# Blocks of 64 rows, high and low parts in one stationary operand, for an expert's rows beyond 128

## What is computed

```
eid = gid[:, None] * MOE_EXPERTS_PER_GROUP + top_i       # T x 2 experts
...
slot_tok = jnp.full((n_slots,), T, dtype=jnp.int32).at[dest].set(stok)
slot_w = jnp.zeros((n_slots,), jnp.float32).at[dest].set(sw)
...
def expert_block(args):
    toks, e = args
    xb = x_pad[toks]
    h = jax.nn.silu(xb @ w_eg[e]) * (xb @ w_eu[e])
    return h @ w_ed[e]
...
y = jnp.zeros((T + 1, D_MODEL), jnp.float32).at[slot_tok].add(out.astype(jnp.float32) * slot_w[:, None])
```

## Time and profile before

| what | value |
|---|---|
| median of 3 executions | 2094.23 us (2093.68 to 2094.96) |
| the profiled execution, its own time | 2093.3 us |
| its span in the profile | 2091.6 us |
| TensorE busy | 1989.5 us, 95% of the span |
| VectorE, ScalarE, GpSimd busy | 49%, 37%, 19% |
| mean granted TensorE clock | 0.983 of full |
| router's last part and experts | from 1618 us to the end |

### The profile page before, as it was taken

How to read it: one execution, slowest core, us unless ns; L and a number is a source line. 1 busy time by engine, 2 the same in 40 slices (tenths; PEclk the granted TensorE clock), 3 DMA queues, 4 the chain that set the end, 5 groups by cost and what they waited for, 6 DMA issues and landing times. The chain is left out here.

```text
span 2091.6 us, 33016 instructions
## 1 busy us (share of the span) xinstructions
PE 1989.5 (95%) x12316; PEld 1764.4 (84%) x12317; DVE 1014.6 (49%) x1166; ACT 776.2 (37%) x1109; POOL 398.2 (19%) x509
## 2 busy tenths in 40 slices
PE   7999999999999999898998999999999899999995
PEld 5788999999888888788997899888788788877884
DVE  4215255543656556465113431435534645784676
ACT  4322122222344344433002222423311456774684
POOL 2000100000444444350110000000000212232224
PEclk9999999999999999899999999999999999999998
DMA  6122233232334343496538021444316486998887
GB/s 197 61 89 68 70 90 94 81 91 82 105 118 125 107 131 103 144 318 236 178 124 278 21 71 30 151 162 162 113 71 224 136 272 194 361 381 270 296 289 278
DMA packets 247474, 333.01 MB, mean 159 GB/s; under 512 B 16269, under 2 KB 163629, under 8 KB 247329
## 3 DMA queue, kind: packets, MB, share of 16 engines
q1 hardware_dynamic: 211268, 276.25, 39.3%
q0 software_dynamic: 7344, 25.38, 4.7%
q10 hardware_dynamic: 28768, 30.02, 4.1%
HBM read 255.30 MB, written 77.61 MB: 159 GB/s over the span
## 5 line engine op out<-in xcount | busy, mean ns | idle before, releaser
L3877 ACT ACTIVATE e_w_high<-big 128x2048 fp32r<-128x2048 f32 x94 | 175.9, 1909 | 36.4 <-PEq L3012 18.0
L274 PE MATMUL psum<-hT_high,t_w_high 128*128 128x352 f32 x576 | 186.9, 324 | 0.3 <-DVE t_w_low L1017 0.3
L276 PE MATMUL psum<-hT_high,t_w_low 128*128 128x352 f32 x576 | 185.6, 322 | 0.0
L275 PE MATMUL psum<-hT_low,t_w_high 128*128 128x352 f32 x576 | 185.6, 322 | 0.0
L4004 DVE TENSOR_TENSOR e_w_low<-big,e_w_high 128x2048 fp32r<-128x2048 f32 x64 | 144.0, 2288 | 37.9 <-ACT e_w_high L3877 37.8
L3781 PE MATMUL psum<-e_w_high,e_xT_high 128*128 128x512 f32 x368 | 146.0, 397 | 8.3 <-issue 5.1
L3782 PE MATMUL psum<-e_w_low,e_xT_high 128*128 128x512 f32 x368 | 144.1, 392 | 0.0
L3783 PE MATMUL psum<-e_w_high,e_xT_low 128*128 128x512 f32 x368 | 144.1, 392 | 0.0
L274 PE MATMUL psum<-hT_high,s_w_high 128*128 128x352 f32 x384 | 131.3, 342 | 0.0
L275 PE MATMUL psum<-hT_low,s_w_high 128*128 128x352 f32 x384 | 124.2, 323 | 0.0
L276 PE MATMUL psum<-hT_high,s_w_low 128*128 128x352 f32 x384 | 124.1, 323 | 0.0
(11 more groups left out here) (570 smaller groups left out, 4885.2 us busy)
## 6 DMA issues: line engine op xcount, KB each, us to landing
big<-in_w_expert_gate SPq DMA_DIRECT2D x32, 1024.0 KB, 8.1
big<-in_w_expert_up SPq DMA_DIRECT2D x32, 1024.0 KB, 11.4
big<-in_w_expert_down SPq DMA_DIRECT2D x32, 1024.0 KB, 13.8
t_w<-in_w_in SPq DMA_DIRECT2D x24, 512.0 KB, 4.8
m_gates<-gate_scr SPq DMA_DIRECT2D x22, 528.0 KB, 5.7
x_scr<-t_conv_out ACTq DMA_DIRECT2D x20, 512.0 KB, 4.3
gate_scr<-s_gate_tanh ACTq DMA_DIRECT2D x16, 528.0 KB, 3.3
scan_w<-in_w_gate SPq DMA_DIRECT2D x16, 512.0 KB, 4.2
```

The lines of the kernel that those rows point to most:

```text
L274: nc.tensor.matmul(out, ah, w_h, start=start, stop=False)
L275: nc.tensor.matmul(out, ah, w_l, start=False, stop=False)
L276: return nc.tensor.matmul(out, al, w_h, start=False, stop=stop)
L3877: return nc.scalar.activation(dst, src, ACT.Copy)
```

## The change

Beyond its first 128 slots, an expert's slots now go in blocks of 64, which run ahead of the expert's full block. In such a block the 64 tokens sit in the even lanes. High and low parts of the turned rows lie in one tile `xhl` (128 x 8 x 2 x 128), and reading it with a step of 2 gives 128 stationary columns: 64 high, 64 low. So gate and up take 2 matmuls per contraction tile (with the high and with the low weights) in place of 3; PSUM then holds the high part's product in partitions 0 to 63 and the low part's in 64 to 127, and VectorE adds the two halves. The down product is unchanged. Experts 0 and 15 keep `hidden` for all of their blocks. The tables grow from 34 to 48 columns, since more blocks are possible. VectorE's `h_low` waits for the down parts in place of TensorE's `down`.

```diff
-NBLK = (2 * T + P - 1) // P + NE
+XR = 64
+NTHR = (T - P + XR - 1) // XR
+NBLK = NE + (2 * (T - P) + 2 * (XR - 1)) // XR + 1
...
-            ch.done(ts(nbk[:], nbk[:], 1.0, None, ALU.max))
-            ch.done(tt(low[:], low[:], mid(nbk[:], NE), ALU.mult))
+            nc.vector.tensor_copy(m.more[:], nbk[:])
+            ch.done(nc.vector.scalar_tensor_tensor(low[:], mid(nbk[:], NE), 1.0, low[:], ALU.add, ALU.mult))
...
+            ts(m.behind[:], base[:], -1.0, 0.0, ALU.add, ALU.max)
...
-        xh = g.sb("e_xT_high", [P, DK, P], F32R, ctx=ctx)
-        xl = g.sb("e_xT_low", [P, DK, P], F32R, ctx=ctx)
+        xhl = g.sb("e_xT", [P, DK, 2, P], F32R, ctx=ctx)
+        xh, xl = xhl[:, :, 0, :], xhl[:, :, 1, :]
...
-            with eng.Fori(0, NE - 1) as e:
-                expert(e, False)
+            expert(0, False, False)
+            with eng.Fori(1, NE - 1) as e:
+                expert(e, True, False)
             at_last()
-            expert(NE - 1, True)
+            expert(NE - 1, False, True)
...
+            def hidden_split(e, b):
+                pe.wait_ge(s_xl, b + 1)
+                pe.wait_ge(s_sg, b)
+                for bank, p, done in ((GA, 0, s_g), (UP, 2, s_u)):
...
+                        parts = xhl[:, k].rearrange("p a t -> p (a t)")[:, 0:2 * P:2]
+                        nc.tensor.matmul(ps[:, bank, :], parts, wh[:, p + half, at:at + BANK], start=(k == 0), stop=False)
+                        mm = nc.tensor.matmul(ps[:, bank, :], parts, wl[:, p + half, at:at + BANK], start=False,
+                                              stop=(k == DK - 1))
+                    mm.then_inc(done, 1)
+                turn(b + 1)
...
-            with pe.Fori(0, NE - 2) as e:
-
-                b = within(start(pe, e) + more(pe, e))
-                hidden(e + 1, b + 1)
-                down(e, b)
+            with pe.Fori(1, NE - 1) as e:
+
+                behind = pe.value_load(m.behind[0:1, bass.ds(e, 1)], min_val=0, max_val=NBLK)
+                n = more(pe, e)
+                with pe.If(n > 0):
+                    with pe.Fori(0, n) as i:
+                        b = within(behind + i)
+                        hidden_split(e, b + 1)
+                        down(b)
+                        turn_h(b + 1)
+                b = within(behind + n)
+                hidden(e, b + 1)
+                down(b)
                 turn_h(b + 1)
-                others(e + 1, b + 1, lambda b: down(e + 1, b))
...
+            def silu_split(b):
+                act.wait_ge(s_gs, b + 1)
+                nc.scalar.activation(sg[0:XR], sg[0:XR], ACT.Silu).then_inc(s_sg, 1)
...
             def gated(b):
+                for s in (s_gl, s_gs, s_ul, s_us):
+                    dve.sem_inc(s, 1)
...
+            def gated_split(b):
+                dve.wait_ge(s_g, b + 1)
+                nc.vector.tensor_copy(sg[0:XR], ps[XR:P, GA, :]).then_inc(s_gl, 1)
+                dve.wait_ge(s_gl, b + 1)
+                nc.vector.tensor_tensor(sg[0:XR], sg[0:XR], ps[0:XR, GA, :], ALU.add).then_inc(s_gs, 1)
+                dve.wait_ge(s_u, b + 1)
+                dve.wait_ge(s_ht, b)
+                nc.vector.tensor_copy(hh[0:XR], ps[XR:P, UP, :]).then_inc(s_ul, 1)
+                dve.wait_ge(s_ul, b + 1)
+                nc.vector.tensor_tensor(hh[0:XR], hh[0:XR], ps[0:XR, UP, :], ALU.add).then_inc(s_us, 1)
+                dve.wait_ge(s_us, b + 1)
+                dve.wait_ge(s_sg, b + 1)
+                nc.vector.tensor_tensor(hh[0:XR], hh[0:XR], sg[0:XR], ALU.mult).then_inc(s_h, 1)
```

More of the change, by code:

```diff
@@ L3144, in _ @@
             nc.gpsimd.memset(valid[0:NS, NC:NT], 1.0)
+            nc.gpsimd.tensor_scalar(step[:], step[:], 2.0, None, ALU.mult)
             nc.gpsimd.affine_select(low[:], low[:], [[1, NE], [-1, NE]], ALU.is_ge, 0.0, 0, 0).then_inc(s_c2, 1)
@@ L3469, in _ @@
             ch.done(nc.vector.tensor_copy(slot_i[:], slot))
-            ch.done(ts(lane_i[:], slot_i[:], P - 1, None, ALU.bitwise_and))
+            for i, bits in enumerate((XR - 1, MORE - XR, BASE - MORE, 64 * BASE - BASE)):
+                op = ts(field_i[:, i], slot_i[:], bits, None, ALU.bitwise_and)
+            ch.done(op)
             wt_all = wt[:].rearrange("p k c -> p (k c)")
-            nc.vector.tensor_copy(inl[:], lane_i[:]).then_inc(s_inl, 1)
-            ch.done(nc.vector.tensor_copy(wth[:], wt_all))
+            ch.done(nc.vector.tensor_copy(field[:], field_i[:]))
+            in_64, of_64, extras, first_at = (field[:, i] for i in range(4))
+            ts(half[:], of_64, float(XR), float(XR), ALU.is_equal, ALU.mult)
+            ts(inl[:], of_64, float(XR), 1.0, ALU.is_gt, ALU.add)
+            ts(past[:], of_64, -float(P), 0.0, ALU.add, ALU.max)
+            nc.vector.tensor_copy(wth[:], wt_all)
+            ch.done(nc.vector.scalar_tensor_tensor(blk[:], of_64, float(XR), extras, ALU.is_le, ALU.mult))
+            ch.done(tt(inl[:], inl[:], in_64, ALU.mult))
+            tt(inl[:], inl[:], half[:], ALU.add).then_inc(s_inl, 1)
+            nc.vector.scalar_tensor_tensor(blk[:], blk[:], float(BASE // MORE), first_at, ALU.mult, ALU.add)
+            ch.done(tt(wtl[:], wt_all, wth[:].bitcast(F32), ALU.subtract))
             dve.wait_ge(s_inl, 1)
-            tt(wtl[:], wt_all, wth[:].bitcast(F32), ALU.subtract)
-            ch.done(tt(blk[:], slot, inl[:], ALU.subtract))
+            ch.done(nc.vector.scalar_tensor_tensor(blk[:], past[:], float(BASE // XR), blk[:], ALU.mult, ALU.add))
             tt(ge[:, :, 0:NCOL], last(blk[:], NCOL), mid(step[:, 0:NCOL], PAIRS), ALU.is_equal).then_inc(s_ge, 1)
@@ L3598, in within, with expert @@
             return nc.s_assert_within(b, 0, NBLK - 2, skip_runtime_bounds_check_because=(
-                "an expert's blocks are at most its slots over 128 and one more, NBLK - 1 in all"))
+                "an expert has one block of 128 slots and one of 64 for each 64 slots begun beyond it, NBLK - 1 in all"))
         def each_block(eng, plain, last_of, at_last):
-            def expert(e, final):
+            def expert(e, split, final):
                 first, n = start(eng, e), more(eng, e)
@@ L3793, in hidden, with down @@
                 turn(b + 1)
-            def down(e, b):
+            def hidden_split(e, b):
+                pe.wait_ge(s_xl, b + 1)
+                pe.wait_ge(s_sg, b)
+                for bank, p, done in ((GA, 0, s_g), (UP, 2, s_u)):
+                    if bank == UP:
+                        pe.wait_ge(s_h, b)
+                    for k in range(DK):
+                        half = k // (DK // 2)
+                        if k % (DK // 2) == 0:
+                            pe.wait_ge(s_wl, e * GU + p + half + 1)
+                        at = (k % (DK // 2)) * FF
+                        parts = xhl[:, k].rearrange("p a t -> p (a t)")[:, 0:2 * P:2]
[4 more added lines that the diff above has]
+                turn(b + 1)
+            def down(b):
                 pe.wait_ge(s_hl, b + 1)
@@ L3800, in down @@
                 for j in range(2):
-                    mm = product(DN + j, hth, htl, 4, FK, D, j * BANK,
-                                 lambda i: pe.wait_ge(s_dl, e * DW + 1 + i))
+                    mm = product(DN + j, hth, htl, 4, FK, D, j * BANK, lambda i: None)
                     if j == 0:
@@ L3860, in _ @@
             hidden(NE - 1, b + 1)
-            down(NE - 2, b)
+            down(b)
             turn_h(b + 1)
@@ L3949, in last_high, with plain @@
                     copy_(wh_l[:, i, :], raw_l[:, i, :]).then_inc(s_dh, 1)
-            def plain(e, i, b, final):
-                silu(b)
+            def plain(e, i, b, split, final):
+                if split:
+                    silu_split(b)
+                else:
+                    silu(b)
                 turned(b + 1)
@@ L3958, in plain @@
                         down_parts(e)
-                h_high(b)
+                if split:
+                    h_high_split(b)
+                else:
+                    h_high(b)
             def last_of(e, n, b, final):
@@ L4022, in down_parts, with plain @@
                                             ALU.subtract).then_inc(s_dl, 1)
-            def plain(e, i, b, final):
-                gated(b)
+            def plain(e, i, b, split, final):
+                if split:
+                    gated_split(b)
+                else:
+                    gated(b)
                 turned(b + 1)
@@ L4029, in plain @@
                         down_parts(e)
-                h_low(b)
+                    dve.wait_ge(s_dl, e * DW + DW)
+                if split:
+                    h_low_split(b)
+                else:
+                    h_low(b)
             def last_low():
@@ L4128, in __init__ @@
         self.more = g.sb("more", [P, NE], I32, ctx=ctx)
+        self.behind = g.sb("behind", [P, NE], I32, ctx=ctx)
 def build(nc, d, out, stages=99):
```

53 lines of the change are left out of this document (36 added, 17 removed).

## The result

| | median | lowest to highest | executions |
|---|---|---|---|
| changed kernel | 2083.04 us | 2082.24 to 2087.36 | 5 |
| kernel before, same chip | 2094.96 us | 2093.68 to 2099.43 | 5 |

The median is 11.9 us lower; the ratio is 0.9941, with a 95% interval of 0.9927 to 0.9955. The profiled execution took 2082.6 us.

A forecast was written before the change was run, and what follows sets the result against it. TensorE was taken to bound the early experts, DMA landings of weights the single-block ones. Savings of 13.5 us less 3.9 for the router and 0.9 small costs gave 8.7 us less: median 2085.5 us, 8-in-10 range 2077 to 2092.

The forecast's parts named there:

- expert 12: Block 18: a ScalarE split already waits for a landing, so later loads stay put; 0.3 us saved, between 0 and 3.6.
- the router: On the path before any gather: more small operations, wider one-hot tables and table matmuls add 3.9 us (2.9 to 4.7).
- experts 1 to 3: Blocks 2, 4 and 6, paced by TensorE: 10.9 us saved, less 1.1 for block 6's landing, so 9.8.
- experts 9 and 10: Block 13 saves 0, waiting for a landing; block 15, whose down split did not wait, saves 3.4 us.
- small costs: Extra semaphore increments, a wait in `h_low` and a register load per expert on TensorE: 0.9 us added in all.
- What the split blocks save: In six blocks, 16 fewer TensorE matmuls at 0.2265 us each save 3.62 us per block, if the strided operand loads equally fast.
- The third rival: The strided operand loads slowly, at 0.376 us, in split blocks: 9.6 us more, 2103.8 us; chance 0.10.
- VectorE's five operations: Five per split block replace one of 0.69 us; hidden while TensorE has work, otherwise 1.4 us lost per block.
- The test that the prediction set itself: Last landing of weights should come some 9 us before 2050; moving by TensorE's whole gain would show the prediction wrong.
- Everything is won: Rival: TensorE paces all six split blocks, so every saving counts; 17.8 us less, 2076.4 us; chance 0.13.
- The landings take most: Rival: weight loads keep experts 1 to 3 and 10 to half their savings; 2.4 us less, 2091.8 us; chance 0.13.
- It doesn't do what it says: Rival: expert counts would give no expert a small block, or several; chance 0.02.

The follow-up runs named there:

- a4: Changed kernel with expert 0's second block split too and expert 0 back inside ScalarE's and VectorE's loops; ratio 0.9933 to the kernel before.
- b2: Changed kernel with split blocks for experts 1 to 8 only, full products from expert 9 on; ratio 0.9955 to the kernel before.
- a3: Changed kernel with no split blocks, every block keeping its full hidden products; 2097.82 us, ratio 1.0005 to the kernel before.
- a2: Kernel before, with only expert 0 written out ahead of ScalarE's and VectorE's loops; 2094.11 us, ratio 0.9983 to the kernel before.
- c3: Changed kernel with the split blocks' stationary operand read as 128 contiguous columns, low parts' product left out; one execution, 2080.48 us.
- b1: Changed kernel with expert 0's second block split too, expert 0 staying ahead of the loops; ratio 0.9904 to the kernel before.
- b4: b1 with 58 dummy matmuls in place of 32 on TensorE ahead of the router's table matmuls; 2074.72 us, ratio 0.9886 to the kernel before.
- a1: Changed kernel run again, unaltered; 2081.71 us, ratio 0.9933 to the kernel before.
- c2: a4 with half the columns of each weight piece loaded from expert 1 on, so outputs differ; ratio 0.9875 to the kernel before.
- c4: Changed kernel with router tables for 33 blocks in place of 47; ratio 0.9938 to the kernel before.

## Why the prediction was right, point by point

The forecast was 8.7 us less and 2085.5 us, in a range of 2077 to 2092; measured were 11.9 and 14.0 less. The range held. Most terms were close. Those that were off (expert 12, the router) were off to the same side, and so was the one that was absent, the table loads. Nothing in the prediction allowed for that one; that it was small enough to stay inside the range is luck. As an estimate of the change with its table loads, a4's 14.0 us less the 3.3 of its extra split block (expert 0: 29.0 - 25.7) leave 10.7, nearer to the 8.7.

| term | predicted us | measured us | from |
|---|---|---|---|
| experts 1 to 3 | -9.8 | -10.4 | profiles; b2 -10.5 |
| experts 9 and 10 | 0 and -3.4 | -3.1 together | experts 4 to 10, seven profiles with splits there, three without |
| expert 12 | -0.3 | -2.6 (2.2 to 3.4) | blocks 16 to 22, the same profiles |
| router and small costs | +3.9, +0.9 | +4.6 (2.1 to 7.1) | a3 against a2; profiles +2.7 to +3.1 to block 0 |
| table loads | not seen | -3.5 (1.7 to 5.2) | a2 |

**What the split blocks save.** The step was 16 x 0.2265 = 3.62 us; it is 3.44 (17.73 - 14.29), 0.17 less. The operand was held to load at the same rate, and it does nearly: 196 ns, and starts are 0.2315 apart, 5 ns more. The 38 ns that a start is longer than a load are no free room, then: 8 ns more in a load showed at once as 5 in a start. c3 shows both gone with the stride. The third rival expected loads of 0.376 us, 0.188 more than a contiguous one; measured were 0.008 more. The Trainium skill (SBUF — State Buffer, Door 1: The DMA port swizzle) gives full rate for two hits in a 16-byte line; the measured 196 ns against 188 is close to that and not quite it, and the measurement decides.

**Experts 1 to 3.** Predicted: 10.9 minus 1.1 that block 6's landing would take. Measured: 10.4, and 3 x 3.44 = 10.3. The landing took nothing; blocks 7 to 11 are 17.70 each. The step that failed is that a late split of ScalarE's delays TensorE; here it had room. The prediction's sign for this term came true: counted from block 0's transposes, ScalarE's split behind expert 9's landing came 9.6 us earlier than before (250.0 us for 259.6).

**VectorE's five operations.** In the changed kernel no wait of TensorE ends with their result. VectorE's timeline of block 2, the rows for the earlier trace rows:

```profile
1687.78 0.69 DVE L4086 COPY e_silu<-psum 64x512 f32<-64x512 f32 x1 [1.68 <-PE psum L3839]
1688.50 0.68 DVE L4088 TENSOR_TENSOR e_silu<-e_silu,psum 64x512 f32<-64x512 f32 x1
1691.51 0.69 DVE L4091 COPY e_h<-psum 64x512 f32<-64x512 f32 x1 [2.33 <-PE psum L3839]
1692.24 0.68 DVE L4093 TENSOR_TENSOR e_h<-e_h,psum 64x512 f32<-64x512 f32 x1
1692.95 0.69 DVE L4096 TENSOR_TENSOR e_h<-e_h,e_silu 64x512 f32<-64x512 f32 x1
```

Five times 0.69, ended at 1693.6, while TensorE had work until its transposes of hidden values at 1697.81. The prediction named the price without that cover, 1.4 us. b1 and b4 have a block without it: block 0 of expert 0, whose transposes have no down product behind them. TensorE's row in b4, whose number in brackets is the wait for VectorE's product:

```profile
1660.50 0.66 PE L3880 MATMUL psum<-ident,e_h 128*128 128x128 f32 x4 [1.34 <-DVE e_h L4112]
```

The wait of 1.34 us stands in b1 as well.

**Experts 9 and 10.** Predicted 3.4 and measured 3.1 (experts 4 to 10: a mean of 144.0 us in the seven profiles with blocks 13 and 15 split, few table loads and full loads of weights, 143.0 to 144.8; 147.0 in a2, a3 and b2, 146.3 to 147.5). How it divides over blocks 13 to 15 differs from one execution to the next (block 15 takes 18.9 us in one profile of the changed kernel and 15.7 in the other). The sum fits the prediction's 0 for block 13 and nearly all for block 15; which block gave it isn't shown.

**Expert 12, the step that failed.** The prediction held that block 18 would only let a later block wait: ScalarE's split at 1989.82 waited for a landing, what is released behind it and the loads up to 2050 would stay. Blocks 16 to 22 take 124.3 us in a2 and a3, 124.1 in b2, and 120.8 to 122.1 in the seven profiles with block 18 split: 2.2 to 3.4 of the 3.44 are kept, where 0.3 was predicted. The landing did get in the way as described: in the changed kernel's profile ScalarE's split waits 1.85 us for it (0.56 before), and TensorE waits 0.59 us in block 20. But the work behind the landing was shorter by a table load. In a4, which has the loads, nothing of block 18 is kept in its one profile. So, as far as that profile goes, the step held for a kernel with its table loads, and they were gone. ScalarE behind expert 9's landing, where the same shows, for the earlier trace rows:

```profile
1898.00 1.91 ACT L3932 ACTIVATE e_w_high<-big 128x2048 fp32r<-128x2048 f32 x1 [3.72 <-DMA big<-in_w_expert_down]
1899.81 0.38 ACT L3932 ACTIVATE e_hT_high<-psum 128x256 fp32r<-128x256 f32 x1
1900.08 0.58 ACT L3951 ACTIVATE e_silu<-psum 128x512 f32<-128x512 f32 x1
```

Silu comes 2.1 us after the split begins, and came 3.7 after it.

The test that the prediction set itself went against it: the last landing should have moved by 9 us and not by the whole gain of TensorE, and it moved by 13.3 (2050.40 to 2037.12), though this profile began the router 4.5 us later. Counted from block 0's transposes it moved by 20.8, and six blocks at 3.44 are 20.6. Yet the split blocks did only part of that. In a3, which has none, it had moved by 7.5 already (a2: 5.8), with the table loads gone. That leaves 13.3 for the split blocks (15.5 in a1), near the 12.6 that the prediction's 8.7 and 3.9 for the router make. The sign spoke for the absent term more than against the landings.

The stream of last loads, from its first issue to its last landing, took 52.0 us before, 50.7 and 50.2 in a2 and a3, 49.4 and 50.4 in the two profiles of the changed kernel. So a DMA share of 1.03 was not quite loads at their limit. And the landing at the end of the earlier trace rows has no cost that shows in what follows the last transposes: that takes 39.1 to 41.5 us in all columns of the table, whether the chain runs through the landing or not.

**The router.** Rows for the earlier trace rows:

```profile
1622.59 0.41 DVE L3464 TENSOR_TENSOR o_over<-o_counts,o_thresholds 128x240 f32<-128x240 f32 x1
...
1627.15 0.41 DVE L3483 TENSOR_SCALAR o_slot_fields<-o_slot 128x18 int32<-128x18 int32 x4
...
1629.17 1.08 DVE L3499 TENSOR_TENSOR o_reached<-o_block_at,o_steps 128x864 f32<-128x864 f32 x1
...
1631.46 2.48 DVE L3502 TENSOR_TENSOR o_block_onehot<-o_reached,o_weights_high 128x864 fp32r<-128x864 f32 x1
1633.87 1.05 DVE L3504 TENSOR_TENSOR o_block_onehot<-o_reached,o_value 128x864 fp32r<-128x864 f32 x1
```

```profile
1635.06 4.09 PE L3275 MATMUL psum<-o_block_onehot,o_lane_onehot 128*128 128x144 f32 x18 [5.79 <-DVE o_block_onehot L3504]
```

The small operations take 2.02 us (1627.15 to 1629.17) for 0.85: +1.2, predicted 1.3. Counts to slots +0.3, predicted 0.4. The one-hot operations up to the matmuls +1.2, predicted 1.2; the third took 2.48 for 1.80, +0.68, predicted 0.7. Its twin without that wait, in the last VectorE row above, takes 1.05 for the same 864 values. GpSimd's timeline has what runs beside it:

```profile
1630.33 2.71 POOL L3174 TENSOR_TENSOR o_block_onehot<-o_reached,o_weights_low 128x864 fp32r<-128x864 f32 x1
```

GpSimd's product ends at 1633.04, VectorE's 0.90 us later, at 1633.94. For this the Trainium skill (SBUF — State Buffer, Who interferes with whom) spoke of a VectorE instruction with two SBUF inputs against GpSimd's reads; the trace agrees with it, and the proportional price was right where the uncontended one (0.3) wasn't.

The matmuls were the miss: 4.09 us for 4.05 in spite of 144 columns for 102, where 1.0 was taken. The term belonged at the low end of its bounds. Together this is +2.7, predicted 3.9.

**The table loads, the term that was absent.** The compiled orders shown ahead of the prediction are VectorE's, and neither they nor the prediction say anything of ScalarE's, in which the loads are gone from the loop. Their price was in the trace too: in the earlier trace rows a split waits 1.87 us for a landing, and silu begins 3.71 us after it. The Trainium skill (ScalarE activation tables: per-element evaluation and per-set limits, Table sets in the compiler and the runtime) says that the compiler places table loads block by block. The runs agree as far as they go: 22 loads with expert 0 in the loops (before, a4, c2), 2 with it outside (the rest). Why the loop needs none when its first turn stands ahead is not shown. The same skill (ScalarE: Activation LUTs, What ACT_TABLE_LOAD costs) has 1.28 us for the load and another 1.38 for a drain, at each switch to a different set. The trace shows the 1.283 us, and silu 1.29 us after the load's start (1985.59 to 1986.88 in a4), so no drain here; and as the peeled loops go without these loads, they were of the set already in use.

**The rivals.** "Everything is won" (2076.4) was nearer to the mechanism than its chance of 0.13 says: blocks 2, 4 and 6 gave their whole saving, 18 gave 2.2 to 3.4 of 3.44, and 13 and 15 together 3.1 of 6.9. "The landings take most" and "the strided operand loads slowly" fell. "It doesn't do what it says" fell with the 96 matmuls.

**What stays open.** a3 against a2 gives 4.6 us and the profiles 2.7 to 3.1 up to block 0. The rest, 1.5 us, may be the small costs (0.9 predicted) or chance; the interval of 2.1 to 7.1 doesn't tell. Nor is it shown which wait turned half of the saving of blocks 13 and 15 away.

## What to carry to other kernels

Read the compiled order of every engine for what the diff doesn't say, and ScalarE's table loads first: an `activation` in a hardware loop may reload its table in each turn; here, writing the first turn out ahead of the loop removed twenty loads. A DMA share of 1.0, or a landing in the chain, doesn't prove that loads pace the kernel; ask what frees their buffers and whether TensorE waits. And look at the granted clock behind TensorE's waits: here it came back at half clock after 3.11 and 5.85 us idle, and filler work that covered the wait kept it at full.

## What the runs showed of the hardware

- A stationary operand read with a step of 8 bytes loads in 196 ns, a contiguous one in 188 (f32, 128 columns); starts go from 0.2265 to 0.2315 us.
- 18 table matmuls took 4.05 us with 102 columns (before) and 4.09 with 144 (b1), both at a granted clock of 0.50; 3.78 with 102 at 0.54 (c4); 2.40 with 144 at full clock (b4). The width hardly sets their pace at these sizes.
- Identical code ahead of the router took 1609.7 (c2) to 1617.5 us (c4) in the 14 profiles, with stretches at a granted clock below full in some and not in others. One profile against another is uncertain by several us in this kernel.
- TensorE's starts were 0.43 us apart for about 3 us behind some waits (a4 at 1996.9, granted clock 0.50) and not behind others: b1 and b4 have the same waits of 1.34 and 0.66 us in block 0, and only b4 slowed after them (0.65 from 1664 to 1667; b1 has 1.00 from 1665 to 1668).
- A VectorE product with two inputs in SBUF took 2.48 us beside a GpSimd product of the same shape and 1.05 without it (864 values), 1.80 and 0.78 with 612 (c4).
